# Three reorderings joined in a two-block transformer kernel: norm transposes by row tile, block 2's mixer, and its head loop

## What is computed

```python
# first_block
for layer in range(2):
    h = rmsnorm(x, attn_norm[layer])
    # layer 0: h @ w_in_even -> fox attention (8 heads) and top-64 sparse attention (8 heads)
    # layer 1: h @ w_in_odd  -> 16 attention heads
    x = x + mixed @ w_out
    x = x + conv_glu_ffn(rmsnorm(x, ffn_norm[layer]), w_up, conv_w, conv_b, w_down)   # 1024 -> 2*2816 -> 1024
x = rmsnorm(x, final_norm)
# second_block
h = rmsnorm(x, norm_mix_g)
c_q, c_kv, k_r, x_m, z, i_pre, f_pre = split(h @ w_in)
attn = 8 "mla" heads on q = rmsnorm(c_q) @ w_uq, kv = rmsnorm(c_kv) @ w_ukv, with rope
xc = silu(causal_conv(x_m)); 4 "mlstm" heads on xc @ w_mq, xc @ w_mk, x_m @ w_mv with gates i_pre, f_pre
ml_out = (layernorm(heads) * mh_norm_g + ml_skip * xc) * silu(z)
x = x + concat(attn, ml_out) @ w_o
x = x + hier_moe(rmsnorm(x))            # 32 experts, top 2 of a token
x = x + (p @ w_ple) * sigmoid(rmsnorm(x) @ w_ple_gate)
return rmsnorm(x, final_norm_g)
```

## Time and profile before

| | us |
|---|---|
| runs of the kernel, three | 1128.29, 1123.03, 1125.15 (median 1125.15) |
| the profiled execution | 1126.01 |
| its span in the trace | 1124.2 |
| PE busy | 1056.7 (94%) |
| DVE busy | 619.9 (55%) |
| ACT busy | 522.5 (46%) |
| granted PE clock, mean | 0.965 |

### The profile page before, as it was taken

How to read it: one execution, slowest core, us unless ns; L and a number is a source line. 1 busy time by engine, 2 the same in 40 slices (tenths; PEclk the granted TensorE clock), 3 DMA queues, 4 the chain that set the end, 5 groups by cost and what they waited for, 6 DMA issues and landing times.

```text
span 1124.2 us, 15541 instructions
## 1 busy us (share of the span) xinstructions
PE 1056.7 (94%) x6143; PEld 828.0 (74%) x6143; DVE 619.9 (55%) x1167; ACT 522.5 (46%) x901; POOL 89.5 (8%) x104
## 2 busy tenths in 40 slices
PE   6998899999999999999999998888989999999987
PEld 5776679999987877789999887678764544555445
DVE  4667356888845555567888647545672121221146
ACT  5654446555535454455555435655352222222155
POOL 0100000212100311001212101100000000000000
PEclk9998699999999999999999999989889999999989
DMA  8733044465565533246565564105628999999930
GB/s 285 272 113 113 1 142 156 155 200 173 190 199 172 187 118 108 76 133 192 164 192 183 191 186 136 76 13 182 229 107 323 409 409 408 409 409 408 406 129 38
DMA packets 112672, 224.63 MB, mean 200 GB/s; under 512 B 10559, under 2 KB 65234, under 8 KB 112594
## 3 DMA queue, kind: packets, MB, share of 16 engines
q1 hardware_dynamic: 112434, 223.04, 56.3%
q10 hardware_dynamic: 160, 0.53, 0.1%
HBM read 222.50 MB, written 1.05 MB: 199 GB/s over the span
## 4 chain that ended last, share of the span: by engine, by line
PE 81%; DVE 9%; ACT 4%; issue 2%; DMA 2%; SPq 1%; POOL 0%; DVEq 0%; ACTq 0%; POOLq 0%
PE ps L525 76%; PE ps L529 4%; DVE wl L1757 2%; ACT wh L1249 1%; DMA ring<-in_w_uv_dram 1%; DVE smb L1771 1%; DVE x L1757 1%; ACT pb L1246 1%; SPq L2627 1%; DMA ring<-in_w_in_even_dram 1%; DVE sA L1767 1%; DVE xs L1757 0%; DVE hl L1767 0%; SPq L2624 0%; ACT L1246 0%
## 5 line engine op out<-in xcount | busy, mean ns | idle before, releaser
L1757 DVE TENSOR_TENSOR wl<-ring,wh 128x1024 fp32r<-128x1024 f32 (+3 forms) x212 | 278.5, 1323 | 183.2 <-ACT wh L1249 182.5
L1249 ACT ACTIVATE wh<-ring 128x1024 fp32r<-128x1024 f32 (+3 forms) x212 | 222.7, 1053 | 155.5 <-PE ps L525 152.5
L525 PE MATMUL ps<-hh,wh 128*128 128x256 f32 x768 | 220.2, 287 | 3.7 <-DVE big L1762 2.3
L525 PE MATMUL ps<-hh,wl 128*128 128x256 f32 x768 | 217.9, 284 | 0.0
L525 PE MATMUL ps<-hl,wh 128*128 128x256 f32 x768 | 217.9, 284 | 0.0
L525 PEld LDWEIGHTS ps<-hh,wh 128*128 128x128 f32 x768 | 147.9, 193 | 5.0 <-DVE wl L1757 2.6
L525 PEld LDWEIGHTS ps<-hl,wh 128*128 128x128 f32 x768 | 147.9, 193 | 0.3
L525 PEld LDWEIGHTS ps<-hh,wl 128*128 128x128 f32 x768 | 147.9, 193 | 0.0
L525 PE MATMUL ps<-wh,hh 128*128 128x512 f32 (+3 forms) x192 | 81.0, 422 | 6.2 <-DVE wl L1757 4.8
L525 PE MATMUL ps<-ring,xg 128*64 128x512 f32 x320 | 85.5, 595 | 0.0
L2578 POOL TENSOR_TENSOR fs<-fs,rt 128x256 f32<-128x256 f32 x44 | 52.5, 1213 | 331.1 <-ACT fs L1246 331.1
(11 more groups left out here) (273 smaller groups left out, 1731.9 us busy)
## 6 DMA issues: line engine op xcount, KB each, us to landing
ring<-in_w_up_dram SPq DMA_DIRECT2D x88, 512.0 KB, 4.7
ring<-in_w_down_dram SPq DMA_DIRECT2D x22, 1024.0 KB, 4.9
ring<-in_w_gate_e_dram SPq DMA_DIRECT2D x40, 512.0 KB, 7.8
ring<-in_w_up_e_dram SPq DMA_DIRECT2D x40, 512.0 KB, 10.1
ringx<-in_w_down_e_dram SPq DMA_DIRECT2D x16, 1024.0 KB, 9.0
ring<-in_w_down_e_dram SPq DMA_DIRECT2D x16, 1024.0 KB, 10.9
ring<-in_w_in_odd_dram SPq DMA_DIRECT2D x12, 1024.0 KB, 5.0
ringx<-in_w_gate_e_dram SPq DMA_DIRECT2D x24, 512.0 KB, 10.1
```

The source lines that it names most:

```text
L525: return e.matmul(o, l, r, start=start, stop=stop)
L1249: return e.activation(o, i, ACT.Copy)
L1757: return e.tensor_tensor(o, a, b, op)
```

## The change

1. **Norms by row tile.** PE's `norm_T` does the eight transposes of row tile 0 first and then those of row tile 1; a group is complete with its row tile 1 part. All seven norms take this order. For fn0, fn1, an1 and nm2 the banks are fixed (`norm_banks`), and the FFN's projections, its output (banks 0, 1, 4, 5) and `xm` (2, 3, 0, 1) use other banks, so that a norm's first groups have banks that the adds do not hold. On DVE the split of the second chunk after an output projection moves behind `add_x`.
2. **Around `pj`, and the mixer.** ACT and DVE split chunk 5 of `w_in` (the argument is 5: chunks up to index 4) before the norm's square root is awaited. One more split is left behind it; on DVE it comes after `pj` is drained. DVE does the taps of head tiles 0 and 1, then the `cum2` copies, then taps 2 and 3 between its two `q2T` copies; ACT's second Silu moves behind its `mv` and first `q2T` copies.
3. **Head loop of block 2.** `z_steps` spreads out to step 14. ACT copies out the probabilities of head i-2 before it takes head i's exponentials, DVE does `ml_2` before the chunk split, and the Silu of z comes after the loop.

```diff
@@ -500,7 +500,7 @@
-        z_steps = (0, 2, 4, 6, 8, 9, 10, 11)
+        z_steps = (0, 2, 4, 6, 8, 10, 12, 14)
@@ -541,14 +541,21 @@
-                for i in range(4):
-                    for t in range(2):
+                for t in range(2):
+                    for i in range(4):
-                    b = claim(i, name, i) if name in ("fn0", "fn1") else take(name, i)
-                    for j in range(4):
-                        k, t = 2 * i + j // 2, j % 2
-                        w = tr(b[:, j * P:(j + 1) * P], x[:, t, k * P:(k + 1) * P])
-                    w.then_inc(of(full, name, i), 1)
+                        if t == 0:
+                            if name in norm_banks:
+                                claim(norm_banks[name][i], name, i)
+                            else:
+                                take(name, i)
+                        b = bank[use[name, i][0]]
+                        for k in (2 * i, 2 * i + 1):
+                            o = (k % 2) * S + t * P
+                            w = tr(b[:, o:o + P], x[:, t, k * P:(k + 1) * P])
+                        if t == 1:
+                            w.then_inc(of(full, name, i), 1)
@@ -619,7 +626,9 @@
-            def out_steps(name, c0, ks, K, xh_, xl_, ready):
+            norm_banks = {"fn0": (4, 5, 0, 1), "an1": (6, 7, 2, 3), "fn1": (4, 5, 0, 1), "nm2": (6, 7, 2, 3)}
+            def out_steps(name, c0, ks, K, xh_, xl_, ready, banks4=(0, 1, 2, 3)):
@@ -631,7 +640,8 @@
-                            b = claim(2 * t + n, name, t, n) if k == 0 and first else bank[2 * t + n]
+                            o = banks4[2 * t + n]
+                            b = claim(o, name, t, n) if k == 0 and first else bank[o]
@@ -645,8 +655,8 @@
-            def out_proj(name, c0, K, xh_, xl_, ready):
-                for _ in out_steps(name, c0, range(K), K, xh_, xl_, ready):
+            def out_proj(name, c0, K, xh_, xl_, ready, banks4):
+                for _ in out_steps(name, c0, range(K), K, xh_, xl_, ready, banks4):
@@ -869,8 +879,9 @@
-                            (0, 1, 2, 3) if s % 2 else (4, 5, 6, 7), lambda: next(side, None))
-                out_proj(("ffo", l), c_ffn[l] + 44, 22, ffh, ffl, lambda k: q.wait_ge(s_ff, 11 * l + k // 2 + 1))
+                            (0, 1, 4, 5) if s % 2 else (2, 3, 6, 7), lambda: next(side, None))
+                out_proj(("ffo", l), c_ffn[l] + 44, 22, ffh, ffl, lambda k: q.wait_ge(s_ff, 11 * l + k // 2 + 1),
+                         (0, 1, 4, 5))
@@ -977,7 +988,7 @@
-            gemm_fm("xm", "nm2", c_in2[1], hh3, hl3, wh, wl, (0, 1, 2, 3), lambda: next(side, None))
+            gemm_fm("xm", "nm2", c_in2[1], hh3, hl3, wh, wl, (2, 3, 0, 1), lambda: next(side, None))
@@ -1540,13 +1551,13 @@
             act(junk[:, 1, :], x[:, 1, :], ACT.Square, accum_out=st[:, 1:2]).then_inc(s_sq, 1)
+            split_hi(c_in2[0] + 5, wh)
-            for c in range(4):
-                split_hi(c_in2[0] + c + 3, wh)
+            split_hi(c_in2[0] + 6, wh)
             tok_evac("pj", pj[:, 1, :], "nm2", 424)
@@ -1585,15 +1596,17 @@
-            for m in range(2):
+            def swish(m):
+            swish(0)
-            for i in (1, 3):
-                evac(flat(qT3[0:96, 2 * i:2 * i + 2, :]), "q2T", i, rows=96)
-            filled(q, "q2T", 3)
+            evac(flat(qT3[0:96, 2:4, :]), "q2T", 1, rows=96)
+            swish(1)
+            evac(flat(qT3[0:96, 6:8, :]), "q2T", 3, rows=96)
@@ -1602,6 +1615,8 @@
+                if 2 <= i < 14:
+                    evac_P(32 + i - 2, ptb3)
@@ -1615,16 +1630,13 @@
-                if 2 <= i < 14:
-                    evac_P(32 + i - 2, ptb3)
-                if i == 13:
-                    for m in range(4):
-                        emptied(q, "z", m)
-                    act(szT[:, :, :], szT[:, :, :], ACT.Silu).then_inc(s_sz, 1)
+            for m in range(4):
+                emptied(q, "z", m)
+            act(szT[:, :, :], szT[:, :, :], ACT.Silu).then_inc(s_sz, 1)
@@ -2098,9 +2110,10 @@
-            for k in range(4, 8):
+            for k in range(4, 7):
             add_x((0, "out"))
+            split_lo(c_ffn[0] + 2, wh, wl)
@@ -2140,9 +2153,10 @@
-                for j in range(18):
+                for j in range(17):
                 add_x(("ffo", l))
+                split_lo(c0 + 4 * 12 + 20, wh, wl)
@@ -2189,9 +2203,10 @@
-            for k in range(4, 8):
+            for k in range(4, 7):
             add_x((1, "out"))
+            split_lo(c_ffn[1] + 2, wh, wl)
@@ -2201,6 +2216,7 @@
+            split_lo(c_in2[0] + 5, wh, wl)
@@ -2211,9 +2227,8 @@
-            for c in range(4):
-                split_lo(c_in2[0] + c + 3, wh, wl)
             tok_evac("pj", pj[:, 0, :], "nm2", 424)
+            split_lo(c_in2[0] + 6, wh, wl)
@@ -2254,7 +2269,7 @@
-            for m in range(4):
+            def taps(m):
@@ -2262,6 +2277,9 @@
+            taps(0)
+            taps(1)
@@ -2270,6 +2288,7 @@
+                taps(2 + i // 2)
@@ -2335,10 +2354,10 @@
+                if 1 <= i <= 12 and order2[i - 1][0] == "ml":
+                    ml_2(order2[i - 1][1], 32 + i - 1)
-                if 1 <= i <= 12 and order2[i - 1][0] == "ml":
-                    ml_2(order2[i - 1][1], 32 + i - 1)
```

## The result

The changed kernel takes **1114.2 us** (median; 1109.5 to 1114.8), the kernel before 1124.7 beside it: a ratio of 0.989, 95% interval 0.986 to 0.993. The forecast was 1116.0 in 1110.5 to 1122.0. The profiled execution took 1114.45 with a span of 1112.6, 11.6 less than before's 1124.2.

A forecast was written before the change was run, and what follows sets the result against it. PE was busy 1056.7 of 1124.2 us, so only its idle or lower-clock stretches could gain. Terms -3.55 + 0.2 + 0.8 + 0.1 - 3.6 - 1.45 - 1.6 = -9.1 us gave a median of 1116.0 us, range 1110.5 to 1122.

The forecast's parts named there:

- Norms, -3.55: At fn0, an1, fn1 and nm2, earlier adds and transposes by row tile shorten PE's waits: -3.55 us in sum.
- Rival (c): New transpose order at the norms is no gain: -0.4 us each for four norms, total 1120.5 us; chance 0.10.
- np2, +0.8: At np2, six more transposes before group 0 delay ACT's hh and PE's gate products: +0.8 us, bounds 0 and +2.5.
- further half-speed stretch: At np2, another stretch at the lower clock, given as the case behind the upper bound of +2.5 us.
- an0, +0.1: At an0, group 0 comes 1.3 us later, but the w_uv load wait does not hang on PE's order: +0.1 us.
- pj to xm, -3.6: Before xm, PE's wait goes (-2.2 us) and the clock fall behind it (about 1.4): -3.6 us.
- Mixer, -1.45: In block 2's mixer, earlier cum2 copies end PE's 2.89 us wait; the last abT group then waits: -1.45 us.
- Head loop, -1.6: In block 2's head loop, the 2.63 us wait goes, new waits come at i = 6 and 10: -1.6 us net.
- my own mark, 46 us: Prediction is wrong if the head loop takes over 46 us from first score to the transposes of its output.
- Rival (b): No clock fall in the head loop or tail: 1.3 us come back, out projection wins some 2; 1112.5 us; chance 0.14.
- (a): Head loop gives back what the mixer wins: loop +1.5, mixer -0.5, sum -5.1 us, total 1120 us; chance 0.14.
- (d): Slower: the clock falls where it held, chiefly in stretches after each norm: +4.2 us, median 1129.5 us; chance 0.04.

The follow-up runs named there:

- joined kernel: The kernel before with all three parts of the change together, that is the changed kernel; 1114.2 us, 0.989 of before; run once more unchanged, 1114.1 us.
- deferred split: The changed kernel with DVE's half of the chunk split one step later in block 2's head loop, behind the next head's maxima; 1110.9 us, 0.986 of before.
- loop part alone: The kernel before with only the head loop edits of the change; 1121.5 us, 0.997 of before.

## Why the prediction was right, and where not

- **Norms, -3.55 (measured -3.98).** The sum was near, the reason half wrong. "Row tile 0's eight transposes follow the last matmul at once" is true, but it was not what gained: the adds start early because the split went behind them (0.83 of 1.1). The ten transposes ahead of group 0 are a cost, 0.3 to 0.5 at each norm. Rival (c) named that cost and overrated it. `hh` came 1.1 earlier (1.60 behind the last matmul's start, 2.71 before), and the first product 3.2 behind its end, for 1.0 and 3.3 worked out.
- **np2, +0.8 (measured -1.3).** That the order costs something was right: from the first transpose to the first product 0.7 at full clock, and 1.1 at half clock (4.40 in the second trace of the joined kernel, 3.30 before), as worked out. The clock was not: it fell there before and in the second trace of the joined kernel and did not in the first, and my "bounds 0 and +2.5" left out a gain. With a fall the term is too small: np2 to the end takes 36.3 to 36.5 us in four traces with the new order, with 10.2 at half clock, and 34.1 to 34.3 in three with the old order, with 6.8. That is +2.1, the "further half-speed stretch" of the upper bound; whether the order brings it is not shown. PE's wait behind the branch is 2.58 us now, nearer to a fetch stall as the Trainium skill has it (Runtime: NRT & Kernel Launch, Instruction fetch mechanics) than to the 108 ns of its page Advanced Engine Details and Errata (Control Flow Timing). The traces show the wait and not its cause.
- **an0, +0.1 (-0.6).** The first product came 1.2 later, as worked out. Of the w_uv load I said that it does not hang on PE's order. DVE got it 0.98 later, but PE's product behind it starts 0.5 and 0.9 later in two kernels with the old order too, so the order need not be to blame; what moves it stays open. PE waited 0.81 instead of 2.16 there and a stretch at half clock behind it fell away.
- **pj to xm, -3.6 (-3.85).** The wait of 2.3 and its cause were right. That 1.4 of clock go with it was taken as sure; it holds in three of four traces with the wait.
- **Mixer, -1.45 (-1.7).** The chain of DVE's taps, Silu and the last q2T copy came out as worked; I missed the 0.82 ahead of the second q2T pair.
- **Head loop, -1.6 (-1.6).** The waits at i = 6 and 10 were 1.02 and 2.06 for my 1.5 and 2.4, their cause is shown by the deferred split, and the 2.63 went. By my own mark, 46 us, the loop was 0.2 too long. PE reached step 5 only 1.1 us earlier after the first score, not 2.65: 3.4 us more at half clock lie ahead of it. The -1.6 itself is luck in part: against the old loop in two other traces it is -1.1 and -0.4, and at equal clock nothing measurable. What I did not see: the copy on ACT, to which I gave only a small cost at the end, costs 1.4 at equal clock, and `ml_2`'s move is worth 3.3 in its company (one run), not 2.63. The terms of a chain do not stand alone.
- **Clock.** Rival (b), no fall in loop or tail, didn't come: 6.8 us at half clock in the loop and 6.8 behind it. The step that fails is that I took falls of the clock in one trace as fixed. +3.0 in layer 1's heads was in no term, nor were the -2.1 at np2, -1.2 ahead of the experts, -0.7 at the start and -0.6 in the experts' stage beyond my terms; together -1.6 of the 2.5 by which the sum was short. The total's closeness to the forecast owes something to their cancelling. Rivals (a) and (d) did not come.

## What to carry to other kernels

Price an edit by the distance between the same two matmuls in two traces: here it repeats to 0.05 us where the clock is the same, while single runs of one program spread over 3 to 14 us with the clock. Where falls of the clock may be part of what an edit does, though, only many runs show it. Where a queue holds work that nobody needs yet and that itself waits for another engine, put it behind what the critical chain needs next; that took 6.9 us off the loop's 46 in one trace and 3.2 off the kernel's median. When several moves arrive together, undo each alone: of these, one order of transposes and one early copy cost a part of what others had won.

## What the runs showed that I had not expected

Which stretches run at half clock differs between executions of one program: 10.3 us or 3.4 in layer 1's first heads, none or 10.2 at np2. The mean over many executions differs between kernels, from 77 us before to some 67 with the loop part alone. Behind the same wait of 2.27 us ahead of xm the clock fell in three kernels and held in one. Mean clock and time go together within each kernel (the deferred split: 1101.1 at 0.978, 1115.0 at 0.966), at 0.35 us for each us at half clock. That is less than half of it. PE is busy in 66.2 of the 81.5 us at half clock of before's trace, which would leave 0.41 as an estimate; what makes up the rest is not shown.
